# A decoder layer with a mixture of experts: the last two projection tiles interleaved by halves, a per-tile expert choice, row splits moved to another engine

## What is computed

```
h = h + merged @ w_out
u = rms_norm(h, norm_ffn_g)
group_logits = u @ w_rg + b_rg                     # 4 groups
g_idx = argmax(group_logits)
exp_logits = (u @ w_re + b_re)[group g_idx]        # 8 of 32 experts
top_v, top_i = top_k(exp_logits, 2)
gates = max(softmax(group_logits)) * softmax(top_v)
h = h + sum over the two experts of gates * ((silu(u @ w_gate) * (u @ w_up)) @ w_down)
```

## Time and profile before

| | |
|---|---|
| median of three runs | 886.07 us |
| the profiled execution | 886.23 us |
| its span, first to last instruction | 884.5 us |
| TensorE busy | 836.7 us (95%) |
| VectorE busy | 342.2 us (39%) |
| ScalarE busy | 273.0 us (31%) |
| GpSimd busy | 82.1 us (9%) |
| moved by DMA | 253.85 MB |

### The profile page before, as it was taken

The page is one execution under the profiler, slowest core; times in us unless marked ns, Lnnn a source line. Parts: engine busy times, 40 slices in busy tenths (PEclk is TensorE's granted clock), DMA queues, the critical chain, the costliest instruction groups (busy, mean ns, idle before and its releaser), DMA issues.

```text
span 884.5 us, 10432 instructions
## 1 busy us (share of the span) xinstructions
PE 836.7 (95%) x4321; PEld 527.9 (60%) x4321; DVE 342.2 (39%) x479; ACT 273.0 (31%) x401; POOL 82.1 (9%) x64
## 2 busy tenths in 40 slices
PE   5999999999999999999999999888998898999996
PEld 4888888788888887536535354352352352533685
DVE  6899549962651616511020120101100101015865
ACT  7666346733332226202010100101001001002777
POOL 3436380000000000000000000000000000001000
PEclk9999999999999999999999999999899999999999
DMA  9222222211525764899999999999999999998902
GB/s 260 97 93 96 95 96 96 96 49 49 189 96 207 296 257 179 349 423 425 401 428 426 428 426 429 426 428 428 428 428 428 426 425 430 427 421 347 356 2 95
DMA packets 45334, 253.85 MB, mean 287 GB/s; under 512 B 8868, under 2 KB 9960, under 8 KB 31976
## 3 DMA queue, kind: packets, MB, share of 16 engines
q1 hardware_dynamic: 42696, 248.21, 69.2%
q0 software_dynamic: 2304, 4.20, 1.2%
q10 hardware_dynamic: 288, 0.79, 0.2%
HBM read 246.89 MB, written 10.49 MB: 291 GB/s over the span
## 4 chain that ended last, share of the span: by engine, by line
PE 44%; DMA 14%; issue 1%; DVE 1%; ACT 1%; DVEq 0%; ACTq 0%
PE bank L1459 42%; DMA ring<-in_w_down_e_dram 11%; DMA ring<-in_w_gate_e_dram 3%; PE bank L1689 1%; PE bank L1785 0%; ACT L1046 0%; ACT r_rounded L901 0%; PE bank L1529 0%; DVE pick L1250 0%; DVE r_rounded L439 0%; ACT r L999 0%; ACT L999 0%; ACT junk L887 0%; PE bank L1775 0%; ACT gain L895 0%
## 5 line engine op out<-in xcount | busy, mean ns | idle before, releaser
L1459 PE MATMUL bank<-ring_rounded,ring_rounded 128*128 128x512 f32 (+1 forms) x696 | 245.0, 389 | 0.3 <-DVE ring_rounded L1134 0.3
L1459 PE MATMUL bank<-r_rounded,ring_rounded 128*128 128x512 f32 (+1 forms) x744 | 234.4, 389 | 0.7 <-DVE ring_rounded L1081 0.6
L1459 PEld LDWEIGHTS bank<-r_rounded,ring_rounded 128*128 128x128 f32 x744 | 138.9, 188 | 30.4 <-DVE ring_rounded L1081 0.9
L1459 PEld LDWEIGHTS bank<-ring_rounded,ring_rounded 128*128 128x128 f32 x696 | 130.3, 188 | 28.1 <-issue 1.3
L1459 PE MATMUL bank<-ring,gain 128*64 128x512 f32 x472 | 118.0, 604 | 9.3 <-issue 8.1
L1459 PE MATMUL bank<-ring,hT 128*64 128x512 f32 x400 | 112.3, 624 | 6.7 <-DMA ring<-in_w_down_e_dram 6.7
L1459 PE MATMUL bank<-ring,junk 128*64 128x512 f32 x472 | 115.5, 592 | 0.0
L1459 PEld LDWEIGHTS bank<-ring,gain 128*64 128x64 f32 x472 | 36.1, 138 | 76.3 <-issue 73.5
L1459 PEld LDWEIGHTS bank<-ring,junk 128*64 128x64 f32 x472 | 37.6, 137 | 71.4 <-issue 71.3
L730 POOL DMA_INDIRECT expert_rows<-r,row_i x16 | 16.5, 1032 | 669.3 <-DVE r L1346 669.3
L945 ACT ACTIVATE r<-bank,factor 128x512 f32<-128x512 f32 x16 | 11.0, 687 | 215.2 <-PE bank L1459 215.2
(11 more groups left out here) (226 smaller groups left out, 761.6 us busy)
## 6 DMA issues: line engine op xcount, KB each, us to landing
ring<-in_w_up_e_dram SPq DMA_DIRECT2D x29, 2048.0 KB, 29.6
ring<-in_w_gate_e_dram SPq DMA_DIRECT2D x24, 2048.0 KB, 27.9
ring<-in_w_down_e_dram SPq DMA_DIRECT2D x22, 2048.0 KB, 32.0
ring<-in_w_in_dram SPq DMA_DIRECT2D x18, 1024.0 KB, 7.3
r<-in_w_gate_e_dram SPq DMA_DIRECT2D x5, 2048.0 KB, 27.9
r<-in_w_down_e_dram SPq DMA_DIRECT2D x4, 2048.0 KB, 34.2
ring<-in_w_down_e_dram SPq DMA_DIRECT2D x7, 1024.0 KB, 21.6
ring<-in_w_up_e_dram SPq DMA_DIRECT2D x6, 1024.0 KB, 11.0
```

The costliest lines, as they stand in the source:

```text
L1459: return nc.tensor.matmul(*a, **k)
```

## The change

- The last two tiles of the last block run side by side: first half of both (g = 0), then second half of both. The transposes, scores, logits and places of the routing are put at fixed products among them.
- The row tiles' choice is made one at a time (`route(i)`), by the instructions that give the eight largest values of a row and their positions: once for the group (the four group logits are padded to eight with weights 0 and bias -1e30), once for the experts, whose first two positions are the two experts.
- `rows_split` moves from VectorE to GpSimd. ACT rounds the row tiles 1, 2 and 3 later than before.
- The first half of the gather is laid around the scores and logits of the last row tile; the second half takes the high parts of both row tiles first, then the low parts.

```diff
-        def rows_split(dve, i):
-            dve.wait_ge(rows_high_ready, i + 1)
-            dve.wait_ge(rows_psum, 2 * i)
-            nc.vector.tensor_tensor(rows_low(i), h1_by_k(i), rows_high(i), ALU.subtract).then_inc(rows_low_ready, 1)
+        def rows_split(pool, i):
+            pool.wait_ge(rows_high_ready, i + 1)
+            if i >= 1:
+                pool.wait_ge(rows_psum, 2 * i)
+                pool.wait_ge(rows_low_ready, i)
+            nc.gpsimd.tensor_tensor(rows_low(i), h1_by_k(i), rows_high(i), ALU.subtract).then_inc(rows_low_ready, 1)
```

On GpSimd, the fills for the padded logits at the start, and the row splits behind its last split of weights:

```diff
+            nc.gpsimd.memset(wrt[:, :, NG:GW], 0.0).then_inc(pads_ready, 1)
+            nc.gpsimd.memset(brt[:, NG:GW], -BIG).then_inc(pads_ready, 1)
...
             low(5)
+            for i in range(TT):
+                rows_split(pool, i)
```

On ACT, the row tiles 1 to 3 (the loop over row tiles is gone):

```diff
+            act.wait_ge(h1_ready, TT + 2)
+            row_norm(1)
+            copy_row_half(1, 0)
+            copy_row_half(1, 1)
+            copy_scores(1)
+            row_high(1)
+            copy_row_half(2, 0)
+            copy_row_half(2, 1)
+            row_norm(2)
+            copy_scores(2)
+            copy_row_half(3, 0)
+            act.wait_ge(h1_ready, 2 * TT)
+            row_norm(3)
+            copy_scores(3)
+            row_high(2)
+            row_high(3)
```

On VectorE, the new choice and its places in the order:

```diff
+            def route(i):
+                dve.wait_ge(logits_psum, i + 1)
+                after(v.scalar_tensor_tensor(out=lg[:, i, :], in0=bank[LOGITS_BANK[i]][:, i * 64:i * 64 + NL],
+                                             scalar=rstd[:, TT + i:TT + i + 1], in1=brt[:, :], op0=ALU.mult, op1=ALU.add))
+                after(v.max(out=group_top[:, i, :], in_=lg[:, i, 0:GW]))
+                after(v.max_index(out=group_at[:, i, :], in_max=group_top[:, i, :], in_values=lg[:, i, 0:GW]))
+                after(v.tensor_tensor(g4[:, 1, i, :], iota[:, 0:NG], group_at[:, i, 0:1].to_broadcast([P, NG]), ALU.not_equal))
+                after(v.scalar_tensor_tensor(out=el[:, i, :].rearrange("p (g e) -> p g e", g=NG),
+                                             in0=g4[:, 1, i, :].unsqueeze(2).to_broadcast([P, NG, PG]), scalar=-2 * BIG,
+                                             in1=lg[:, i, GW:NL].rearrange("p (g e) -> p g e", g=NG), op0=ALU.mult, op1=ALU.add))
+                after(v.max(out=expert_top[:, i, :], in_=el[:, i, :]))
+                after(v.max_index(out=expert_at[:, i, :], in_max=expert_top[:, i, :], in_values=el[:, i, :]))
+                after(v.tensor_tensor(chosen[:, :, i, :], iota[:, 0:NE].unsqueeze(1).to_broadcast([P, 2, NE]),
+                                      expert_at[:, i, 0:2].unsqueeze(2).to_broadcast([P, 2, NE]), ALU.is_equal))
+                v.tensor_tensor(routed_bf[:, i, :], oh1[:, i, :], oh2[:, i, :], ALU.add).then_inc(routed_ready, 1)
+                v.tensor_tensor(routed[:, i, :], oh1[:, i, :], oh2[:, i, :], ALU.add).then_inc(routed_ready, 1)
...
                     residual(c)
+                    if c == TT + 1:
+                        dve.wait_ge(pads_ready, 2)
+                        for i in range(2):
+                            row_rstd(i)
+                            route(i)
+                    if c == TT + 2:
+                        find_places(0)
...
-            rows_split(dve, TT - 2)
-            row_rstd(TT - 1)
-            route(1)
+            for i in (2, 3):
+                row_rstd(i)
+                route(i)
...
             find_places(1)
-            rows_split(dve, TT - 1)
```

On TensorE, where `products(t, g, meanwhile)` issues the twelve products of one half of tile t, with calls ahead of some of them:

```diff
+            products(LAST_TWO, 0, {6: lambda: transpose_h1(1)})
+            products(LAST_TWO + 1, 0, {2: lambda: scores(1)}).then_inc(first_half_used, 1)
+            products(LAST_TWO, 1, {1: lambda: logits(1)}).then_inc(tile_done, 1)
+
+            def second_tile_turned():
+                transpose_h1(2)
+                places(0)
+
+            products(LAST_TWO + 1, 1, {5: second_tile_turned}).then_inc(tile_done, 1)
...
-            places(0)
-            transpose_h1(TT - 1)
-            keep_busy(6)
-            scores(TT - 1)
-            logits(TT - 1)
+            scores(2)
+            transpose_h1(3)
+            logits(2)
             pe.wait_ge(pick_ready, 1)
             pe.wait_ge(rows_high_ready, 2)
             pe.wait_ge(rows_low_ready, 2)
-            keep_busy(14)
+            gather_first((6, 7))
+            scores(3)
+            gather_first((4,))
+            logits(3)
+            gather_first((5, 0, 1, 2, 3))
             places(1)
             keep_busy(12)
             pe.wait_ge(pick_ready, 2)
-            pe.wait_ge(rows_high_ready, TT)
-            pe.wait_ge(rows_low_ready, TT - 1)
+            for i in (2, 3):
+                pe.wait_ge(rows_high_ready, i + 1)
+                for k in range(KD):
+                    gather_k(bank[4 + k // 2], k, i, (rows_high,), start=False, stop=False)
+            pe.wait_ge(rows_low_ready, 3)
...
```

More of the change, by code:

```diff
@@ L1204, in bc @@
                 return ap.unsqueeze(2).to_broadcast([P, ap.shape[1], n])
[L1206 to L1234, removed]
@@ L1238, in find_places @@
                 dve.wait_ge(places_psum, half + 1)
[L1239 removed]
+                dve.wait_ge(routed_ready, 4 * half + 4)
                 after(v.scalar_tensor_tensor(out=cand[:, at, :],
@@ L1483, in keep_busy @@
                 for _ in range(products):
-                    mm(bank[3][:, 0:P], ones[:, :], before[:, :], start=True, stop=True)
+                    mm(bank[0][:, 0:P], ones[:, :], before[:, :], start=True, stop=True)
             for q in range(2 * TT):
@@ L1565, in places, with products @@
                 ins.then_inc(places_psum, 1)
-            for t, (kind, c) in enumerate(tiles):
-                n = block_of[kind, c]
-                k_tiles = blocks[n][2]
+            def products(t, g, meanwhile=None):
+                kind, c = tiles[t]
+                n = t // 4
                 dst = bank[t % 4][:, :]
+                at = 0
+                for part in ("high", "low"):
+                    for k in range(4 * g, 4 * g + 4):
+                        if t % 4 == 0 and k % 4 == 0:
+                            if part == "high":
+                                pe.wait_ge(high_ready, halves.index((n, g)) + 1)
+                            else:
+                                pe.wait_ge(*lows_at(n, g))
+                        if (kind, c, part) == ("out", 0, "high"):
+                            pe.wait_ge(merged_low_ready, k + 1)
+                        w = (high_half if part == "high" else low_half)(n, g)[:, k % 4, :]
+                        for factor, x_ in enumerate(moving[kind][0:2 if part == "high" else 1]):
+                            if meanwhile and at in meanwhile:
+                                meanwhile[at]()
+                            at += 1
+                            flags = dict(start=(k == 0 and part == "high" and factor == 0),
+                                         stop=(k == blocks[n][2] - 1 and part == "low"))
+                            if kind == "out":
+                                ins = mm(dst, x_(k)[:, (c % TT) * P:(c % TT + 1) * P], w, **flags)
+                            else:
+                                ins = mm(dst, w[:, (t % 4) * P:(t % 4 + 1) * P], x_(k), **flags)
+                return ins
+            LAST_TWO = len(tiles) - 2
+            for t, (kind, c) in enumerate(tiles[:LAST_TWO]):
                 if t == 3:
@@ L1703, in gather_next, with gather_first @@
                 gather()
-            pe.wait_ge(const_ready, 7)
-            places(0)
-            transpose_h1(TT - 1)
-            keep_busy(6)
-            scores(TT - 1)
-            logits(TT - 1)
+            def gather_first(ks):
+                for k in ks:
+                    for i in range(2):
+                        gather_k(bank[4 + k // 2], k, i, start=(i == 0 and k % 2 == 0), stop=False)
+            scores(2)
+            transpose_h1(3)
+            logits(2)
             pe.wait_ge(pick_ready, 1)
@@ L1713, in _ @@
             pe.wait_ge(rows_low_ready, 2)
-            for k in range(KD):
-                for i in range(2):
-                    gather_k(bank[4 + k // 2], k, i, start=(i == 0 and k % 2 == 0), stop=False)
-            keep_busy(14)
+            gather_first((6, 7))
[3 more added lines that the diff above has]
+            gather_first((5, 0, 1, 2, 3))
             places(1)
```

100 lines of the change are left out of this document (39 added, 61 removed).

## The result

The changed kernel takes 890.80 us (median of five runs, 889.37 to 891.42) against 886.07: the ratio is 1.0047, with a 95% interval of 1.0035 to 1.0058. It is slower, by about what was forecast. The profiled execution took 890.32, with a span of 888.5: 4.1 more than the one before.

A forecast was written before the change was run, and what follows sets the result against it. The start of the first gate product (363.31) was taken to bound the kernel. Profiled 886.2, plus 3.0 for waits on GpSimd's splits and 1.6 for the clock, gave 890.8 us; range 881.8 to 894.

The forecast's parts named there:

- the clock: TensorE idling before the last places: half clock over places and part of the gather costs 0 to 2.5 us, 1.6 taken.
- the turns: Choice of row tile 3: third split holds until 356.8, one VectorE instruction passes, fourth holds until 360.1; sum ends 360.5.
- What bounds it: Start of the first gate product, 363.31 before: a microsecond won or lost ahead of it is one of the whole.
- The tiles by halves and the choice: End of routing: half loads near 339, last tile ending at 347.1 instead of 347.5, choice 2.5 us per row tile.
- The wait on the port: VectorE instructions with two SBUF operands wait for GpSimd's split: row tile 1's comparison until 342.1, next transposes until 344.35.
- the port is free: Rival: GpSimd's split holds VectorE much less than its span; gate products at 359.5, 3.8 us earlier, total 882.4; chance 0.20.
- T: Time of one row split on GpSimd: 3.2 us taken, ends 2.3 and 4.6; result moves 3 us per us.
- the extra read: Row split on GpSimd reading h1 with a step of eight words: 0.7 to 1.2 us, added once.

## Why the prediction was right

The time went where the forecast put it: into waits for the splits, and into the clock behind them. One step, the turns, went another way than forecast. The gate products stood at "near 368" in the prediction and at 367.05 in the profile; the sum of 890.8 lies 0.5 above the profiled execution.

- **What bounds it.** The start of the first gate product moved by 3.74 and the execution by 4.1. The kernels above follow it too: in all eleven profiled executions the time is 522.7 to 523.6 more than the start of the first gate product.
- **The tiles by halves and the choice.** First half loads at 339.15 (forecast: near 339), scores of row tile 1 ended by 336.56 (336.4), the last tile by 347.06 (347.1), scores of row tile 3 by 351.32 (351.0). The choice of one row tile takes 2.4 without a wait (2.5 forecast): the eight largest 0.17 to 0.20, each index search 0.09 and 0.16 to 0.19.
- **The wait on the port.** The comparison of row tile 1 was held until 342.2 (forecast 342.1), and the transposes behind the residual until 344.19 (344.35). The rival "the port is free" falls with these rows and with the two runs that held splits back. The condition, two operands in SBUF, was too narrow: a one-operand TENSOR_SCALAR was held too, though not on the path of the changed kernel.
- **T.** 2.85 to 3.08, where 3.2 was taken: the extra read was added to 2.3 at 0.9 and measured 0.50 to 0.67.
- **The turns.** This step was wrong in its detail: "one VectorE instruction passes; the fourth split takes its turn". The forecast has the group comparison of row tile 3 meet the third split at 353.4; it ran at 353.20 and the masking at 353.40, both ahead of that split (353.85), and the expert comparison was the first to be held. Behind it a second instruction passed, because GpSimd restarted 0.17 after its split: the sum for TensorE came at 357.1 and not 360.5. That took the places out of the second wait; the copy of the sums took their place in it and held the pick up. With the smaller T, the pick ended at 361.15 instead of 362.25. By the forecast's own steps 360.5 was too early: the masking, a maximum and an index search, some 0.7 us, stand between the two comparisons and are missing from it.
- **The clock.** 1.6 was taken and 1.8 measured (5.91 against 4.10 with the idle time filled). It varies: the same 32 products took 5.43 to 6.65 in the other runs in which the clock had fallen before them. The idle time was not one stretch of 6 us but two of 2.5 and 3, with short products between them that did not hold the clock.

The 0.85 us between forecast and measured gate product was made up elsewhere: about 0.35 is lost behind that product, and the median lies 0.5 above the profiled execution. For these two no cause was looked for. That the sum meets the median to the last digit is luck: the pick came 1.1 earlier than forecast, and the longer gather, the time behind the gate product and the median above the profiled execution made that up. The range's upper end, 894, is about 1 us above what its terms give (886.2 + 4.2 + 2.5 = 892.9).

## What to carry to other kernels

Before work is moved to an engine that looks idle, list what runs beside it there. Here a subtraction on GpSimd stopped the VectorE instructions that read two tensors from SBUF until it was done, however small they were (a comparison of four columns took 1.82 us instead of 0.16), and a string of tiny instructions on the critical path suffers most. A single operand is no safe pass: one-operand TENSOR_SCALARs were held too. What went through beside a split were instructions with an operand in PSUM, the eight largest, the index searches, a reduction and a reciprocal. In this kernel the last two splits were cheaper on VectorE, behind the end of the string. A wait that leaves TensorE idle can be paid a second time in its clock (1.8 us here), so cost both.

## What the runs showed of the hardware that I had not expected

- A VectorE instruction with a single SBUF operand can be held as well: a TENSOR_SCALAR of 128x4 took 2.01 us instead of 0.17, until the split beside it ended. A TENSOR_REDUCE just before it, beside the same split, took its normal 0.17.
- The hold can end before the GpSimd instruction does: a two-operand comparison took 1.84 us beside a one-operand GpSimd instruction of 3.78.
- GpSimd takes 0.17 us between two of its splits when the second waits for the first, time enough for a VectorE instruction of 0.2 to get through behind the one that was held.
- The granted clock was 0.50 behind idle stretches of 0.96 and 1.90 us with eight products between them (the last two splits held back on GpSimd), and 1.00 behind stretches of 0.62 and 1.02 us with 24 products between them (the last two splits on VectorE).
